# Two-layer encoder and hybrid-attention decoder: the compression weights multiplied as they land, without splitting

## The reference

```python
def nsa_compress(t, gidx, pe, w1, w2):
    B = t.shape[0]
    blocks = t[:, gidx] + pe
    flat = blocks.reshape(B, gidx.shape[0], NSA_CMP_LEN * HEAD_DIM)
    return jax.nn.silu(flat @ w1) @ w2
```

## Time and profile before

| | us |
|---|---|
| median of 3 runs | 1856.4 |
| lowest and highest | 1846.52 and 1856.69 |
| the profiled execution, its own time | 1856.4 |
| its span, first to last instruction | 1854.6 |
| TensorE busy | 1825.6 |
| VectorE busy | 1242.4 |
| ScalarE busy | 978.3 |

### The profile page before, as it was taken

How to read it: one execution, slowest core, us unless ns; L and a number is a source line. 1 busy time by engine, 2 the same in 40 slices (tenths; PEclk the granted TensorE clock), 3 DMA queues, 4 the chain that set the end, 5 groups by cost and what they waited for, 6 DMA issues and landing times.

```text
span 1854.6 us, 35725 instructions
## 1 busy us (share of the span) xinstructions
PE 1825.6 (98%) x15290; PEld 1742.3 (94%) x15290; DVE 1242.4 (67%) x1895; ACT 978.3 (53%) x1493; POOL 67.9 (4%) x32
## 2 busy tenths in 40 slices
PE   7999999999999999999999999999999999999999
PEld 7999998899999999999988999999989989989889
DVE  6775666765766567756667657665776678766676
ACT  6443567355544454445673555444555565656562
POOL 0000011400000000000114000000000000000000
PEclk9999999999999999999999999999999999999999
DMA  8555543233555655555432335555446334446332
GB/s 328 188 186 189 172 156 118 92 126 120 185 184 187 211 182 191 185 184 179 151 118 97 126 114 182 183 189 186 160 159 213 130 112 173 160 148 227 126 111 95
DMA packets 84461, 302.40 MB, mean 163 GB/s; under 512 B 9168, under 2 KB 11728, under 8 KB 84176
## 3 DMA queue, kind: packets, MB, share of 16 engines
q1 hardware_dynamic: 84304, 300.13, 46.4%
HBM read 299.04 MB, written 1.05 MB: 162 GB/s over the span
## 4 chain that ended last, share of the span: by engine, by line
PE 90%; DVE 5%; ACT 3%; issue 1%; DMA 0%; SPq 0%; DVEq 0%; ACTq 0%
PE bank L382 22%; PE bank L385 22%; PE bank L386 22%; PE bank L688 2%; DVE w_lo L1556 1%; PE bank L404 1%; PE bank L403 1%; PE bank L400 1%; PE bank L447 1%; PE bank L451 1%; PE bank L452 1%; PE bank L615 1%; PE bank L1005 1%; PE bank L1056 1%; PE bank L890 1%; PE bank L1026 1%
## 5 line engine op out<-in xcount | busy, mean ns | idle before, releaser
L1556 DVE TENSOR_TENSOR w_lo<-ring,w_hi 128x1024 fp32r<-128x1024 f32 x560 | 678.6, 1247 | 98.1 <-ACT w_hi L1122 97.0
L1122 ACT ACTIVATE w_hi<-ring 128x1024 fp32r<-128x1024 f32 x560 | 580.1, 1054 | 261.2 <-PE bank L382 222.1
L382 PE MATMUL bank<-xs,w_hi 128*128 128x256 f32 x2448 | 694.0, 284 | 0.0
L386 PE MATMUL bank<-xs,w_lo 128*128 128x256 f32 x2448 | 684.8, 280 | 0.0
L385 PE MATMUL bank<-xs,w_hi 128*128 128x256 f32 x2448 | 684.7, 280 | 0.0
L382 PEld LDWEIGHTS bank<-xs,w_hi 128*128 128x128 f32 x2448 | 463.5, 189 | 4.1 <-issue 3.0
L385 PEld LDWEIGHTS bank<-xs,w_hi 128*128 128x128 f32 x2448 | 462.1, 189 | 3.2 <-issue 2.9
L386 PEld LDWEIGHTS bank<-xs,w_lo 128*128 128x128 f32 x2448 | 462.4, 189 | 0.0
L382 PE MATMUL bank<-a,w_hi 128*128 128x256 f32 x704 | 197.8, 281 | 0.0
L385 PE MATMUL bank<-a,w_hi 128*128 128x256 f32 x704 | 197.8, 281 | 0.0
L386 PE MATMUL bank<-a,w_lo 128*128 128x256 f32 x704 | 197.8, 281 | 0.0
(11 more groups left out here) (399 smaller groups left out, 3086.2 us busy)
## 6 DMA issues: line engine op xcount, KB each, us to landing
ring<-in_w SPq DMA_DIRECT2D x560, 512.0 KB, 3.3
arena<-in_mem SPq DMA_DIRECT2D x2, 1024.0 KB, 12.8
const<-in_const SPq DMA_DIRECT2D x1, 1395.0 KB, 15.9
h<-in_x SPq DMA_DIRECT2D x1, 768.0 KB, 7.1
out<-h SPq DMA_DIRECT2D x3, 256.0 KB, 2.5
dec_par<-in_dec SPq DMA_DIRECT2D x1, 615.0 KB, 19.9
h<-in_x SPq DMA_DIRECT2D x1, 256.0 KB, 4.9
out<-h SPq DMA_DIRECT2D x2, 128.0 KB, 2.0
```

What stands on the lines that cost most here:

```text
L382: last = nc.tensor.matmul(o, wh, hi(x, k0 + k), start=k == 0, stop=False, skip_group_check=True)
L386: last = nc.tensor.matmul(o, wl, hi(x, k0 + k), start=False, stop=k == nk - 1, skip_group_check=True)
L1122: nc.scalar.activation(w_hi[:, s * UNIT:(s + 1) * UNIT], ring[:, u % RU, :], AF.Copy).then_inc(sems("w_hi"), 1)
L1556: nc.vector.tensor_tensor(w_lo[:, r * UNIT:(r + 1) * UNIT], ring[:, r, :], w_hi[:, s * UNIT:(s + 1) * UNIT].bitcast(F32), ALU.subtract).th ...
```

## The change

The eight compression units of each layer are no longer split. TensorE waits for their landing itself (`Stream.block`) and multiplies `flat` with the unit as it lies in the ring, as plain float32: one matmul of 30 by 256 for each of the 32 steps in place of three in fp32r. `flat_hi` and `flat_lo` are gone, and with them the memset in the second layer. The slots of `w_hi` are counted over the split units alone (`SPLIT_BEFORE`), so ScalarE and VectorE go on to the gate units while TensorE is in the compression stage. The pad before `arena` and the rounding in `parts` are gone too: `arena` begins at byte 120,544, which is 96 past a multiple of 128. `a`, `xo`, `ob` and `mg` are then 96 past a multiple of 128 (64 before), `ms` is at a multiple of 128 (64 past one before), `yx` and `xs` are 64 past one as before.

```diff
+def whole(u):
+
+    v = u - LAYERS * ENC_UNITS
+    return v >= 0 and U_CMP <= v % DEC_UNITS < U_GL
+
+
+SPLIT = [u for u in range(UNITS_ALL) if not whole(u)]
+SPLIT_BEFORE = [sum(not whole(v) for v in range(u)) for u in range(UNITS_ALL + 1)]
...
-        if (64 - here()) % 128:
-            sb("arena_pad", (64 - here()) % 128 // 4)
...
-            n0 = at[0] = -(-at[0] // 32) * 32
+            n0 = at[0]
...
-                self.w.e.wait_ge(sems("w_lo"), u + 1)
+                self.w.e.wait_ge(sems("w_lo"), SPLIT_BEFORE[u + 1])
+
+            def block(self, wide=1):
+
+                u, pos = divmod(self.n, UB)
+                assert pos + wide <= UB and whole(u)
+                if pos == 0:
+                    self.w.e.wait_ge(sems(f"landed{u % RU}"), 16 * (u // RU + 1))
+                self.n += wide
+                c = pos * P
+                return ring[:, u % RU, c:c + wide * P], pos == 0
...
-                pe.e.wait_ge(*pe.need('flat_lo', 1))
+                pe.e.wait_ge(*pe.need('flat', 4))
                 for l in range(32):
-                    wh, wl, first = w.two(2)
-                    fh, fl = (f[:, l * 2 * NCMP:(l + 1) * 2 * NCMP] for f in (flat_hi, flat_lo))
-                    o = bank[5][0:2 * NCMP, 0:T]
-                    last = nc.tensor.matmul(o, fh, wh, start=l == 0, stop=False, skip_group_check=True)
+                    blk, first = w.block(2)
+                    last = nc.tensor.matmul(bank[5][0:2 * NCMP, 0:T], flat[:, l, :], blk, start=l == 0, stop=l == 31,
+                        skip_group_check=True)
                     if first:
                         last.then_inc(sems("unit_begun"), 1)
-                    nc.tensor.matmul(o, fl, wh, start=False, stop=False, skip_group_check=True)
-                    last = nc.tensor.matmul(o, fh, wl, start=False, stop=l == 31, skip_group_check=True)
-                    if l == 31:
+                    elif l == 31:
                         last.then_inc(*pe.tell('hid_full'))
...
                 for u in range(self.u, min(upto, UNITS_ALL)):
-                    if True:
-                        s = u % HU
+                    if not whole(u):
+                        n = SPLIT_BEFORE[u]
+                        s = n % HU
                         self.w.e.wait_ge(sems(f"landed{u % RU}"), 16 * (u // RU + 1))
-                        if u >= HU:
-                            self.w.e.wait_ge(sems("unit_begun"), u - HU + 2)
+                        if n >= HU:
+                            self.w.e.wait_ge(sems("unit_begun"), SPLIT[n - HU] + 2)
...
-                a.e.wait_ge(*a.need('flat', 4))
-                nc.scalar.activation(tiles(flat_hi[:, :], 32), flat, AF.Copy).then_inc(*a.tell('flat_hi'))
                 for j in range(4):
-                    s.ahead(u0 + U_Z + 2 * j + 2)
+                    s.ahead(u0 + (U_Z + 2 * j + 2 if j < 3 else U_GL))
...
-                for n in range(1, 9):
-                    s.ahead(u0 + U_CMP + n)
+                s.highs(u0 + U_GL + HU)
                 a.e.wait_ge(*a.need('hid_full', 1))
...
-                d.e.wait_ge(*d.need('flat_hi', 1))
-                nc.vector.tensor_tensor(tiles(flat_lo[:, :], 32), flat, tiles(flat_hi[:, :], 32).bitcast(F32),
-                    ALU.subtract).then_inc(*d.tell('flat_lo'))
                 for j in range(4):
-                    w.ahead(u0 + U_Z + 2 * j + 2)
+                    w.ahead(u0 + (U_Z + 2 * j + 2 if j < 3 else U_GL))
                     d.e.wait_ge(*d.need('z_full', j + 1))
...
-
-                for n in range(1, 9):
-                    w.ahead(u0 + U_CMP + n)
```

More of the change, by code:

```diff
@@ L93 @@
               pt="v_sb", f_sq="v_sb", q_sq="ab", q_ln="zl", q_rstd="b_e", masks="l_sb", v="y0", fv="a_sb",
[L94 to L100, removed]
-FFN_UNITS = 3 * KF
+              gf="o_out", gate_e="o_sq", ft="os_out", z_out="os_rstd", hid_s="ys", hid_e="l_sq", kc_sq="gz_e",
+              vc="l_ln", forget_hi="l_rstd", kcs_ln="dte", kcs_rstd="eg", pc_e="yy", gl_s="f_out", ptc="vn",
+              mg_hi="ss", fgain="x_lo", wab="g_r", mx="g_r", half_bg="g_r", qk="ff", pn="ff", zs_in="m_ss",
+              xo_lo="m_ss", wgf="m_ss", gg="m_lo", f_var="m_lo", f_ss="sp_sb", raw="sp_sb", qn="g_out",
+              q_sin="y", qr="gcol", flat="dt", xf="mixed", lf="k_out", z_r="qkn", gl_e="rr", fcol="kb",
+              kcn="kq", kc="kend", pc_d="lt", pcn="qkd", nm="xt_up", ob="x_up", up_out="r1", mgd="mix_lo")
+FFN_UNITS = 3 * KF
+def whole(u):
[3 more added lines that the diff above has]
+SPLIT_BEFORE = [sum(not whole(v) for v in range(u)) for u in range(UNITS_ALL + 1)]
 class Counts:
@@ L224, in build_program @@
         ident, ones, bones, le = C("ident"), C("ones"), C("bones"), C("le")
-        if (64 - here()) % 128:
-            sb("arena_pad", (64 - here()) % 128 // 4)
+        room = (nc.sbuf_bytes_remaining // 4 // 8) * 8 - 64
         arena_at = here()
-        assert ring_at % 128 == 0 and hi_at % 128 == 0 and xs_at % 128 == 64 and arena_at % 128 == 64
-        room = (nc.sbuf_bytes_remaining // 4 // 8) * 8 - 64
         arena = sb("arena", room)
@@ L323, in build_program @@
         obf, ob = parts("ob", 8)
-        at[0] = max(at[0], after_pairs)
+        assert at[0] == after_pairs
         forget_r = rounded("forget", T, arena_at + 4 * at[0])
-        flat_hi = rounded("flat_hi", 64 * NCMP, arena_at + 4 * pairs_at)
         kvc = take(T)
@@ L329, in build_program @@
         zb = take(8, T)
-        flat_lo = rounded("flat_lo", 64 * NCMP, arena_at + 4 * at[0])
         flat, hid, hid_t = take(32, 2 * NCMP), take(2, 2 * NCMP), take(T)
@@ L358, in low_ready @@
             def low_ready(self, u):
-                self.w.e.wait_ge(sems("w_lo"), u + 1)
+                self.w.e.wait_ge(sems("w_lo"), SPLIT_BEFORE[u + 1])
[7 more added lines that the diff above has]
+                return ring[:, u % RU, c:c + wide * P], pos == 0
             def two(self, wide=1):
                 u, pos = divmod(self.n, UB)
-                assert pos + wide <= UB
+                assert pos + wide <= UB and not whole(u)
                 if pos == 0:
@@ L368, in two @@
                 self.n += wide
-                c, d = (u % HU * UB + pos) * P, (u % RU * UB + pos) * P
+                c, d = (SPLIT_BEFORE[u] % HU * UB + pos) * P, (u % RU * UB + pos) * P
                 return w_hi[:, c:c + wide * P], w_lo[:, d:d + wide * P], pos == 0
@@ L1552, in lows @@
                 for u in range(self.u, min(upto, UNITS_ALL)):
-                    if True:
-                        s, r = u % HU, u % RU
-                        self.w.e.wait_ge(sems("w_hi"), u + 1)
+                    if not whole(u):
+                        s, r = SPLIT_BEFORE[u] % HU, u % RU
+                        self.w.e.wait_ge(sems("w_hi"), SPLIT_BEFORE[u + 1])
                         nc.vector.tensor_tensor(w_lo[:, r * UNIT:(r + 1) * UNIT], ring[:, r, :],
@@ L1914, in hybrid_dve @@
                 pe_ = DEC(par, "pe").unsqueeze(2)
-                nc.vector.memset(flat, 0.0).then_inc(*d.tell())
-                d.e.wait_ge(*d.own())
+                if l == 0:
+                    nc.vector.memset(flat, 0.0).then_inc(*d.tell())
+                    d.e.wait_ge(*d.own())
                 for kv in range(2):
```

## The result

The changed kernel takes 1867.25 us (median of 7 runs, 1862.27 to 1868.98) against 1856.37 for the kernel before (7 runs). The two medians are 10.9 us apart. The ratio of the two kernels, taken over all their comparable runs, is 1.0072, with a 95% interval of 1.0059 to 1.0085, which is +13.4 us (11.0 to 15.8). The prediction was 1861.9, +5.5. The time lies in its range, but the loss is two times the one forecast or more.

A forecast was written before the change was run, and what follows sets the result against it. The prediction took TensorE, busy 98% of the span, as the bound. To 1856.4 us it added 5.5 for the float32 compression stages and nothing for all other terms, giving 1861.9, range 1853 to 1868.

The forecast's parts named there:

- What bounds the kernel: Whole kernel: TensorE, busy 98% of the span; relief of ScalarE and VectorE counts only where a TensorE wait shrinks.
- Added to TensorE: Compression stage: 32 float32 matmuls of 0.432 us, 13.8 us for 11.10 in each layer, +5.5 us for both.
- rival E: Compression stage: 30 stationary columns make float32 matmuls cheap, -7.6 us for both layers, 1848.8 us; chance 0.05.
- The landing: Compression stage: TensorE now waits for the units themselves, asked for nine units ahead; cost nothing, at most 1.6 us.
- the moved splits: Gate units made before the last z tiles: fourth z tile at about 1432.7, needed about 1441; cost nothing.
- the relief: ScalarE and VectorE lose eight copies and eight subtractions per layer, beside a TensorE that never stops; counted as nothing.
- the wait at line 974: TensorE's wait of 1.83 us in each layer stays as it is, only 2.7 us later.
- Rival D: Decoder: relief of ScalarE and VectorE counts after all, up to 5.7 us of waits and 1.5 of clock, 1854.7; chance 0.07.
- The arena moves by 96 bytes: Activations at a new place in memory: taken as 0, with 14.7 us either way kept open over 3264 matmuls.
- Rival C: Moved operands a, xo, ob, mg read more slowly, 4.5 ns per matmul, +14.7 us, 1876.6 us; chance 0.07.
- B: Rival: matmul spacing of the moved operands flips from 0.118 to 0.113 us, gain 14.7 us, 1847.2 us; chance 0.07.

The follow-up runs named there:

- e2: The kernel before with only the arena's pad and the rounding in parts removed, compression stage still split: 1863.53 us against 1851.4, ratio 1.0048.
- e4: As e1, with xs and the arena both at a multiple of 128, where the weights stand too: 1897.48 us, ratio 1.0237.
- e10: The changed kernel with four unused float32 transposes in the second to fourth feed-forward: 1854.6 us, ratio to the kernel before 1.0007.
- e3: As e1, with 32 bytes more before xs, so xs stands 96 past a multiple of 128: 1879.87 us, ratio 1.0142.
- e1: The changed kernel with the arena's pad and the rounding put back: 1858.77 us against 1851.4 for the kernel before, ratio 1.0036.
- e6: As e4, but with the weights (ring and w_hi) moved to 64 past a multiple of 128: 1851.7 us, one execution.
- e5: As e1, with xs and the arena 32 past a multiple of 128, weights at 0: 1868.2 us against 1859.05, one execution.
- e9: The kernel before with four unused 128-column float32 transposes in every feed-forward but the first: 1836.15 us, ratio 0.9889.
- e11: As e9, with the transposes in the first feed-forward too and the identity loaded earlier: 1834.36 us, ratio 0.9892.

## Why the prediction was half right

*What bounds the kernel.* Right. TensorE was the whole account: its waits are the same within 0.6 us, and 16 to 21 us of work less on ScalarE and VectorE changed nothing.

*Added to TensorE.* Right in mechanism and size: 13.8 us for each stage were forecast and 13.93 measured. Inside the stage a record took (1436.79 - 1423.60) / 61 = 0.216, as forecast. What I had left out are the longer steps at its two ends, so that the term is +6.0 for both layers against +5.5. Two rows of the same operation at another place were enough, and the 30 stationary columns indeed gained nothing (rival E is out). By the Trainium skill's formula for the gap between matmuls ("TensorE: Matmul & The Clock Gate", section "Back-to-back issue gap") it would have been +7.0. The page calls this the gap of isolated matmuls and says that in a stream of weight loads and matmuls both set the spacing; here the fp32r pairs stand 113 to 118 ns apart where the formula gives 109. The rows were closer.

*The landing, the moved splits, the relief, the wait at line 974.* Right: no idle time before or in the stage, the fourth z tile at 1434.4 (forecast 1432.7; the stage began 1.3 us later than before, and the fourth gate unit landed some 5 us after it was asked for and not 4) against a need at about 1443, and 1.8 us at the wait in both layers. Rival D is out. The clock stayed at 1.00 around that wait in the profiled execution of the changed kernel.

*The arena moves by 96 bytes: "I take 0".* This is the step that failed. The term is +8.9 us by e2 (5.2 to 12.8 by its interval), and 7.5 in the stretches of the moved activations in the profiled executions, where the kernel before happened to be slow in all four feed-forwards. Rival C had the activations (`a`, `xo`, `ob`, `mg`) and the direction, at a chance of 0.07, with 4.5 ns for each matmul. Its condition, a start 32 past a multiple of 64, was not the cause: with the starts at a multiple of 128 e4 pays the same 120 ns. Measured for `a` are 2.2 ns over the slow rhythm and 6.7 over the quick one. My argument against it was that `xs` shows both 113 and 118 from one place, so the place chooses nothing. The first half is true and the conclusion doesn't follow: `a` 96 past the weights showed neither rhythm in any of its 12 stretches (the changed kernel, e2, e10), so the place decides whether they are to be had at all. "No fp32r distance of a long stretch is above 0.118" was no evidence either, since all the long stretches of the kernel before have their operand 64 from the weights.

The second support was the 16-byte cachelines of the Trainium skill ("SBUF — State Buffer", section "Specifications (TRN2)"), from which I concluded that a shift by a multiple of 32 bytes is free. For TensorE e2, e3 and e4 say that such a shift is not free: by their ratios e2 is +8.9 us on the kernel before, and e3 and e4 are +20 and +37 us on e1, and between each pair lies nothing but such shifts.

*B, the rhythm flips by itself.* It does, by 6.8 us for each feed-forward where `a` lies 64 from the weights (e1's first against its others) and by 4.5 where it lies at 96. The kernel before ranged from 1843 to 1862 us over the chips of this study; on one chip 16 us of that are left when the clock is corrected for. That the rhythm makes the rest is likely, but of its executions only one has a profile. The profiled execution of the changed kernel (1862.87) was 4.4 us under the median (1867.25), and its one quick first feed-forward is worth 4.5.

## What to carry to other kernels

Where TensorE is the bound, compare matmul distances from start to start between two traces, stretch by stretch and by operand; a per cent of all matmuls hides in an average, and a profile can sit in a lucky execution. A pad or a rounding in a memory layout is an edit like any other: price it by what lies at what distance from what, not by whether it "computes" anything. For fp32r pairs of moving operand and weights, try starts 64 bytes apart within 128 first. Take a float32 matmul of 256 columns at 0.43 us, more than three fp32r ones (0.35).

## What the runs showed of the hardware that I had not expected

- The distance between fp32r matmuls of 128 x 256 at the 2.4 GHz level depends on the starts of moving operand and weights, taken together, within 128 bytes: 113.3 or 117.8 ns at 64 apart (before, e6), 120 at 0 (e4), 118.4 (`xs`, e3) or 120 (`a`, e2) at 96 against 0, and 117 to 118 at 32 (e5). Why `xs` and `a` differ at 96, and what brings the whole about, was not tried.
- At 64 apart there are two rhythms, and one of them lasts through a whole feed-forward of 187 us. Four small float32 transposes ahead of it went with the quick one in 9 of 9 later feed-forwards (six of them are the second or the fourth, slow in every profile with `xs` 64 from the weights and without the transposes) and won 1.1% (e9).
- The fastest versions are e9 and e11, 0.9889 and 0.9892 of the kernel before, with the split compression stage and the padded arena. They beat both kernels of this study.
